# MLP operands moved by 32 bytes, most of the residual stored earlier, and a wait in front of the last down projection split in two

## The reference

```python
y = jnp.concatenate([y_conv, y_rwkv], axis=-1) @ w_out[i]
h_res = h_res + y
h = rms_norm(h_res, norm_mlp_g[i])
h_res = h_res + jnp.square(jax.nn.relu(h @ w_up[i])) @ w_down[i]
out = rms_norm(h_res, final_norm_g)
return out[:, N_META:]
```

## Time and profile before

| | us |
|---|---|
| median of 3 runs | 2312.63 (2311.72 to 2313.81) |
| the profiled execution | 2299.77 |
| its span, first to last instruction | 2297.7 |
| PE busy in it | 2275.2 (99%) |

### The profile page before, as it was taken

How to read it: one execution, slowest core, us unless ns; L and a number is a source line. 1 busy time by engine, 2 the same in 40 slices (tenths; PEclk the granted TensorE clock), 3 DMA queues, 4 the chain that set the end, 5 groups by cost and what they waited for, 6 DMA issues and landing times.

```text
span 2297.7 us, 53673 instructions
## 1 busy us (share of the span) xinstructions
PE 2275.2 (99%) x21424; PEld 2180.3 (95%) x21424; DVE 1702.4 (74%) x2742; ACT 1113.2 (48%) x2076; POOL 299.3 (13%) x342
## 2 busy tenths in 40 slices
PE   8999999999999999999999999999999999999998
PEld 8999999999999788899999999999999999999988
DVE  7568667577586765578788778788788788787656
ACT  6534444344344423345555545555555455555436
POOL 5102012012020232200100001001001001001007
PEclk9999999999999999999999999999999999999999
DMA  7343343342442653445635536537447447357434
GB/s 245 87 106 82 95 98 83 94 109 78 100 103 72 161 178 89 141 123 134 157 102 138 139 101 157 138 93 165 120 111 165 120 112 172 95 130 200 139 97 152
DMA packets 513318, 286.26 MB, mean 125 GB/s; under 512 B 84526, under 2 KB 490544, under 8 KB 512688
## 3 DMA queue, kind: packets, MB, share of 16 engines
q1 hardware_dynamic: 478512, 224.19, 35.9%
q0 software_dynamic: 24080, 56.20, 10.9%
q10 hardware_dynamic: 10496, 2.62, 0.6%
HBM read 232.47 MB, written 50.47 MB: 123 GB/s over the span
## 4 chain that ended last, share of the span: by engine, by line
PE 87%; DVE 6%; DMA 3%; POOL 1%; issue 1%; ACT 1%; SPq 0%; ACTq 0%; POOLq 0%; DVEq 0%
PE PD L2136 15%; PE PD L2131 10%; PE PW L2384 10%; PE PW L2386 10%; PE PW L2385 10%; PE PD L2385 7%; PE PD L2384 7%; PE PD L2386 7%; PE PD L2350 1%; DVE w_lo L1530 1%; PE PD L2160 1%; PE PW L2160 1%; POOL acc L964 1%; DMA w_raw<-in_w_in 1%; POOL psq L962 1%
## 5 line engine op out<-in xcount | busy, mean ns | idle before, releaser
L2136 PE MATMUL PD<-act_both,w_hi 128*128 128x264 f32 (+1 forms) x2496 | 413.1, 287 | 0.0
L2136 PEld LDWEIGHTS PD<-act_both,w_hi 128*128 128x128 f32 x2496 | 341.6, 188 | 12.0 <-issue 6.7
L2385 PE MATMUL PW<-uf,w_hi 128*128 128x256 f32 x1120 | 312.7, 279 | 0.0
L2386 PE MATMUL PW<-uf,w_lo 128*128 128x256 f32 x1120 | 312.6, 279 | 0.0
L2384 PE MATMUL PW<-uf,w_hi 128*128 128x256 f32 x1120 | 312.6, 279 | 0.0
L1483 DVE TENSOR_TENSOR w_lo<-w_sum,w_hi 128x512 fp32r<-128x512 f32 x352 | 241.6, 688 | 67.3 <-ACT w_hi L1015 66.2
L1530 DVE TENSOR_TENSOR w_lo<-w_raw,w_hi 128x512 fp32r<-128x512 f32 x268 | 200.9, 776 | 101.2 <-ACT w_hi L1031 98.2
L1015 ACT CAST w_hi<-w_sum 128x512 fp32r<-128x512 f32 x352 | 217.7, 619 | 110.7 <-PE PW L2386 87.0
L1031 ACT CAST w_hi<-w_raw 128x512 fp32r<-128x512 f32 x268 | 159.2, 619 | 214.6 <-DMA w_raw<-in_w_in 99.9
L2136 PE MATMUL PD<-act_both,w_lo 128*128 128x264 f32 (+1 forms) x1248 | 250.8, 282 | 0.0
L2384 PE MATMUL PD<-plain,w_hi 128*128 128x256 f32 x768 | 214.5, 279 | 0.0
(11 more groups left out here) (414 smaller groups left out, 5848.4 us busy)
## 6 DMA issues: line engine op xcount, KB each, us to landing
w_raw<-in_w_in SPq DMA_DIRECT2D x200, 256.0 KB, 3.2
w_raw<-in_w_down SPq DMA_DIRECT2D x136, 256.0 KB, 2.9
w_more<-in_w_down SPq DMA_DIRECT2D x136, 256.0 KB, 2.9
w_raw<-in_w_up SPq DMA_DIRECT2D x128, 256.0 KB, 3.1
w_more<-in_w_up SPq DMA_DIRECT2D x128, 256.0 KB, 3.5
residual<-form POOLq DMA_DIRECT2D x56, 512.0 KB, 7.3
w_raw<-in_w_out SPq DMA_DIRECT2D x64, 256.0 KB, 2.9
residual<-res POOLq DMA_DIRECT2D x4, 2048.0 KB, 10.3
```

What stands on the lines that cost most here:

```text
L2136: ins = M(PD[:, 2 * (n % 2) + a, cols], w, v[:, k, start:start + cols.stop - cols.start], start=begin, stop=end)
L2385: M(bank, whi, lo, start=False, stop=False, skip_group_check=True)
L2386: return M(bank, wlo, hi, start=False, stop=end, skip_group_check=True)
```

## The change

Three things are changed. `before_forms` is 8 columns shorter, and `eps_t` becomes the last two columns of `par` instead of a tile of its own behind `ident`. With that every tile behind them, and every tile that the MLP streams, starts 32 bytes lower: 128 bytes behind a multiple of 256. `act_both` and the weight slots stay where they are. Twelve tiles of the residual are stored by POOL between the 14th and the 15th square, the other four where all stood before. And PE waits in front of the last down only for the additions up to the second of the last unit; for the rest it waits ahead of the second tile.

```diff
+STORED_EARLY = 12
-    sb("before_forms", [P, 72], on=over_act)
+    sb("before_forms", [P, 64], on=over_act)
...
-    par = sb("par", [P, PAR_COLS])
+    par = sb("par", [P, PAR_COLS + 2])
+    eps_t = par[:, PAR_COLS:PAR_COLS + 2]
     ident = sb("ident", [P, P])
-    eps_t = sb("eps_t", [P, 2])
...
-            with pool.Fori(0, KT // 2 - 1) as i:
+            with pool.Fori(0, STORED_EARLY // 2 + 1) as i:
                 tile(0, i)
                 tile(1, i)
+            pool.dma_start(res_view[:, 0:STORED_EARLY, :], res[:, 0:STORED_EARLY, :]).then_inc(delta_added[0], 16)
             tile(0, KT // 2 - 1)

         squares(T_OUT, 0)
         pool.wait_ge(evacuated[(T_OUT + KT - 1) % 2], free(T_OUT + KT - 1))
-        for h in range(2):
-            cols = slice(h * KT // 2, (h + 1) * KT // 2)
-            pool.dma_start(res_view[:, cols, :], res[:, cols, :]).then_inc(delta_added[h], 16)
+        pool.dma_start(res_view[:, STORED_EARLY:KT, :], res[:, STORED_EARLY:KT, :]).then_inc(delta_added[1], 16)
...
-        pe.wait_ge(gathered, GATHERED_0 + N_GATHERED * HALF_UT * FFG)
+        pe.wait_ge(gathered, GATHERED_0 + N_GATHERED * (HALF_UT * FFG - 1) + 2)
...
-        for _ in dense(KT, KQ, Q_LAST, T_LAST, u_hi, u_lo, operand=operand, one_bank=range(KT), slots=slots):
-            pass
+        for step_, _ in enumerate(dense(KT, KQ, Q_LAST, T_LAST, u_hi, u_lo, operand=operand, one_bank=range(KT), slots=slots), 1):
+            if step_ == KQ:
+                pe.wait_ge(gathered, GATHERED_0 + N_GATHERED * HALF_UT * FFG)
```

## The result

| | before | changed |
|---|---|---|
| median of 5 runs each, us | 2311.72 | 2328.84 |
| lowest and highest, us | 2299.37, 2313.81 | 2328.25, 2329.87 |
| profiled execution, us | 2299.77 | 2328.25 |
| its span, us | 2297.7 | 2326.2 |

The changed kernel is slower: ratio 1.0095, 95% interval 1.0066 to 1.0125. Span against span the loss is 28.5 us. The kernel before has two kinds of time: its executions, here and beside all the experiments, lie at 2298.6 to 2304.1 us or at 2310.3 to 2315.9 and never between, which is why its median and its profiled execution stand so far from each other; the changed one has a single time.

The account below looks back on a forecast made before the run. PE, 87% of the chain that ended last, was taken as the bound; 2299.8 - 11.4 - 2.3 - 1.1 = 2285.0 us for the profiled execution, with 12.9 for the median 2297.8; range 2277 to 2314.

Parts of the forecast that it names:

- The addresses: Seven-product code and last down: operands starting at 128 instead of 160 make PE's matmuls 0.9% faster, 11.4 us of 1266.
- the step from mixed starts to one start: Output projection's four alternating starts, 231.3 ns against the last down's 233.5, taken as the gain of starting always at 128.
- just twice: At 160, 512 columns cost twice 256 (233.5 against 2 x 116.7 ns), so the 0.9% carries over to 256-column matmuls.
- Rival B: MLP matmuls: 128 is a bad start, streamed operand and PEld's weights collide; 0.9% more, 2320.6 us; chance 0.15.
- Rival A: MLP matmuls: the addresses change nothing, the 0.9% belongs to the alternation of four starts; 2309.2 us; chance 0.27.
- rival C: MLP matmuls: 128 each time is as good as the shortest, 390 ns; 27 us gained, 2282 us; chance 0.14.
- The upper end: Worst case for the operand starts: 128 like the longest `act_both` matmul, 397 against 395 ns, losing 0.9%, 11 us.
- The base: Whole kernel: the median lies 12.9 us above the profiled execution, added to 2285.0 to give 2297.8 us.
- Edit 2: Residual store: 3 MB issued at about 944.1 us remove DVE's wait and PE's 2.1 us wait; gain 2.3 us.
- Rival D: Small edits fail: 3 MB slow the weight loads or another chain holds PE near 989; at most 3.4 us, beside any other.
- Edit 3: Start of the last down: PE no longer waits for two additions, nor at the second tile; gain 1.1 us.
- The near half tiles: Near the end POOL sets the pace and a faster PE only waits, so PE's gain counts only up to the first half tile.

Follow-up runs that it names:

- 160/160: Against the kernel before: weight slots moved to 160 like the operands, early store and split wait in; 2330.61 us, ratio 1.0112.
- 192/160: Against the kernel before: operands moved to 192 and weight slots to 160, early store and split wait in; 2295.63 us in the profile.
- 96 apart: Against the kernel before: operands moved to 224, weight slots left at 128, early store and split wait in; 2331.3 us.
- the small edits: Against the kernel before: early residual store and split wait only, operands left at 160, slots at 128; profiled 2296.0 us, ratio of medians 1.000.
- the execution with five places: Against the small edits alone: `plain1` moved to 64, `uf1` to 96, `plain3` to 32, `uf0` to 0, `hf` and `uf2` left at 160; 2298.16 us.
- the fastest version: Against the kernel before: `plain` and `uf` at 64, `hf` at 160, last down's operands at 128, early store and split wait in; 2269.52 us, ratio 0.9852.

## Why the prediction was wrong

**The addresses** decided it, and the step that failed is the one that the prediction had named as its weakest, "the step from mixed starts to one start", together with the sentence ahead of it, that "the excess goes with the columns and not with the instruction, which lets me carry the difference over to the 256-column matmuls". At 128 the 512-column matmuls did get faster, by 6.5 ns where I had said 2.2. The 256-column ones got slower: the term that stands in the sum as a gain of 11.4 us came out as a loss of 33.6 (34.9 less 1.3). At distance 0 the excess is a fixed 13.3 ns per matmul, 32 cycles, whether it has 256 columns (120.0 less 106.7) or 512 (226.7 less 213.3); at distance 32 it is 10 and 20 ns. The "just twice" was true of one distance only. The output projection stood at a mixture of distances, 0, 64, 128 and 192 in turn, and nothing of it carried over. That two stages differed with clock and shape equal was a sign that places matter, not of which place is better for another shape.

**Rival B** had the mechanism in words, "the streamed operand then lies at the same place behind a multiple of 256 as the weights that PEld reads at the same time". The runs at 160/160 and 192/160 show that the distance to the weights is what counts. It was given a chance of 0.15, and its price was mis-sized: 0.9% of 1266 us, 11.4 us, where the stage lost 34.9 and the last down gained 1.3. I had taken it from the spread of single lengths in the earlier trace rows; they had no row at that distance and that shape. Whether two reads collide there was not measured: a collision at equal places alone would not explain the 120.0 at 96 apart.

**Rival A** fell: 32 bytes were worth 32.3 us with the small edits in (2328.25 less 2296.0 in the profiled executions) and 32.5 without them (2332.3 less 2299.8). The Trainium skill, "SBUF — State Buffer", "Specifications (TRN2)", gives lines of 16 bytes and a penalty for crossing them, which leads to no difference between two starts that are both multiples of 16; the measured 116.67 and 120.0 ns say otherwise. The Trainium skill, "TensorE: Matmul & The Clock Gate", "Step-by-step: what each phase is for", says that the streamed operand and the weight load have independent read ports, and that loading weights takes nothing from the running matmul; the traces of the 160/160 and 192/160 runs disagree: the interval went from 116.67 to 120.0 ns and back with the distance between the two. Which of the two reads is held up they don't show.

**The bounds.** The lower end of rival C, 390 ns, was even passed by the last down (389). The upper end, 0.9%, was the fault in the range: the highest single length among neighbours isn't a bound for a combination that no row shows. A loss of 2.9% (120.0 over 116.67) lay outside all that was priced.

**The base.** I treated the 12.9 us between the profiled execution and the median as an offset that any version would keep. It is the distance between two kinds of time, and a change of place can leave only one of them. For the same reason the opening statement that runs lie within 2.1 us of each other, and the bound of 0.2% drawn from it, held only inside one kind: the 87 executions of the kernel before that these comparisons hold reach from 2298.6 to 2315.9 us.

**Edit 2** was right in its place and nearly in size: the two loads issued at 965.9 and 966.5 land 3.7 and 3.9 us later, DVE's and PE's waits are gone, no other link was late at 990, and the store's issue took 1.06 us. I had said 2.3 us; with the small edits alone the time from the first product of the MLP to the last up matmul is some 2.4 us shorter. Rival D fell.

**Edit 3** was right: 1.0 us, with no wait at the second tile.

**The near half tiles** didn't take up the loss either. POOL's first square of that stage comes at 2263.8 us, 28.5 later than before, and it is 28.5 us that the span grew. POOL waited 44.9 us for it where it had waited 47.3.

## What to carry to other kernels

Measure the distance between an operand's start and the weights' start, modulo 256, for the shape in question, before moving tiles: it is worth 113.3 to 120.0 ns on one float32 matmul of 256 columns, and a figure from 512 columns doesn't carry over. When a kernel's times fall in two groups, compare the groups and look for a stretch that runs in two ways, before taking a median as the base of a sum. Where a place has a good and a bad rhythm, let the sequence enter it from a place that gives the good one; here that made 2269.5 us of 2301.8.

## What the runs showed of the hardware

- With 128x128 weight tiles loaded ahead of every float32 matmul, the interval in cycles at 2.4 GHz is 256 + 32 and 512 + 32 at equal places, 256 + 24 and 512 + 48 at 32 bytes apart, 256 + 16 in the short rhythm at 64 below (120.0, 226.8, 116.67, 233.3 and 113.3 ns).
- At 64 below, the same products take 113.5 or 117.8 ns, shown within one execution twice. At 32 apart they take 116.67 or 117.76, shown within the execution with five places: 116.67 when entered from `uf2` at the same place, 117.76 when entered from `plain3` at 32. Not every other place does this: in the fastest version `hf` is entered from `plain` at 64 and takes 116.7.
- That the 11 us between the two kinds of time of the kernel before are the pair at 32 apart is argued, from 1.1 ns x 10,464: every profile of a version with only that distance fell in the short kind. What chooses at the start of the stage stays open; the one change of rhythm that a trace shows without a change of tile came at a hitch of PE of 0.2 us.
- DMA traffic made no difference to the interval: in the fastest version two stretches of the same `hf` products have 83 of them in 9.40 us, 116.6 ns, under a DMA share of 0.22 and under one of 0.78.

```profile
1122.90:1132.30 9.40, 9.40 (x83) 1.00 0.78 182
```
